# Values mixed in three reduced-precision passes, with steps of the softmax moved forward on VectorE and ScalarE

## What is computed

```python
logits = jnp.einsum('bnqhgd,bnkhd->bnhgqk', qb, kb) * (HEAD_DIM ** -0.5)
logits = jnp.where(valid, logits, -1e30)
probs = jax.nn.softmax(jnp.concatenate([logits, sink_col], axis=-1), axis=-1)[..., :-1]
out = jnp.einsum('bnhgqk,bnkhd->bnqhgd', probs.astype(v.dtype), vb)

rnn = hr * jax.nn.gelu(yr)          # hr: two gated linear recurrences, forward and backward
merged = (jax.nn.sigmoid(ga) * (attn @ w_proj_attn[i])
          + jax.nn.sigmoid(gr) * (rnn @ w_proj_rnn[i]))
```

## Time and profile before

| | us |
|---|---|
| median of three timed runs | 949.85 (949.08 to 950.12) |
| the profiled execution | 949.1 |
| its span, first to last instruction | 947.3 |
| TensorE busy | 927.0 (98%) |
| VectorE busy | 729.6 (77%) |
| ScalarE busy | 577.1 (61%) |

### The profile page before, as it was taken

The page is one execution under the profiler, slowest core; times in us unless marked ns, Lnnn a source line. Parts: engine busy times, 40 slices in busy tenths (PEclk is TensorE's granted clock), DMA queues, the critical chain, the costliest instruction groups (busy, mean ns, idle before and its releaser), DMA issues.

```text
span 947.3 us, 12574 instructions
## 1 busy us (share of the span) xinstructions
PE 927.0 (98%) x5100; PEld 800.1 (84%) x5100; DVE 729.6 (77%) x981; ACT 577.1 (61%) x730; POOL 1.4 (0%) x9
## 2 busy tenths in 40 slices
PE   5999999999999999999999999999999999999996
PEld 3898988988888888888889889888888888888885
DVE  5888898787867867767868698888878676866755
ACT  4578899764356644555345889987435564545540
POOL 0000000000000000000000000000000000000000
PEclk9999999999999999999999999999999999999998
DMA  9546444584485555566443644456656656555521
GB/s 333 153 163 200 136 156 157 185 305 164 156 266 182 199 198 178 192 203 204 160 161 119 211 159 155 134 180 197 256 179 217 226 187 205 186 180 198 201 89 45
DMA packets 118457, 174.62 MB, mean 184 GB/s; under 512 B 3968, under 2 KB 78976, under 8 KB 117888
## 3 DMA queue, kind: packets, MB, share of 16 engines
q1 hardware_dynamic: 118256, 173.79, 55.0%
q10 hardware_dynamic: 144, 0.03, 0.0%
HBM read 172.76 MB, written 1.05 MB: 183 GB/s over the span
## 4 chain that ended last, share of the span: by engine, by line
PE 88%; DVE 7%; ACT 4%; DMA 0%; issue 0%; DVEq 0%; ACTq 0%
PE ring L548 13%; PE ring L550 13%; PE ring L549 13%; PE ring L601 9%; PE ring L597 9%; PE misc L548 5%; PE misc L549 5%; PE misc L550 5%; PE ring L600 5%; PE ring L598 5%; PE misc L778 2%; DVE sb_w_lo L1253 2%; PE ring L721 1%; PE misc L837 1%; ACT sb_w_hi L933 1%; DVE sb_tmp L1485 1%
## 5 line engine op out<-in xcount | busy, mean ns | idle before, releaser
L1253 DVE TENSOR_TENSOR sb_w_lo<-sb_raw,sb_w_hi 128x2048 fp32r<-128x2048 f32 x138 | 294.8, 2148 | 65.8 <-ACT sb_w_hi L933 65.8
L933 ACT CAST sb_w_hi<-sb_raw 128x2048 fp32r<-128x2048 f32 x138 | 246.3, 1796 | 19.6 <-DMA sb_raw<-in_w_out_dram 4.3
L601 PE MATMUL ring<-sb_x_both,sb_w_hi 128*128 128x512 f32 x272 | 107.6, 396 | 0.0
L597 PE MATMUL ring<-sb_x_both,sb_w_hi 128*128 128x512 f32 x272 | 107.5, 395 | 0.0
L548 PE MATMUL ring<-sb_w_hi,sb_x_both 128*128 128x512 f32 x272 | 107.1, 394 | 0.0
L549 PE MATMUL ring<-sb_w_lo,sb_x_both 128*128 128x512 f32 x272 | 106.0, 390 | 0.0
L550 PE MATMUL ring<-sb_w_hi,sb_x_both 128*128 128x512 f32 x272 | 106.0, 390 | 0.0
L600 PE MATMUL ring<-sb_x_both,sb_w_lo 128*128 128x256 f32 x272 | 75.7, 278 | 0.0
L598 PE MATMUL ring<-sb_x_both,sb_w_lo 128*128 128x256 f32 x272 | 75.4, 277 | 0.0
L548 PE MATMUL ring<-sb_x_both,sb_w_hi 128*128 128x256 f32 x256 | 72.6, 284 | 0.0
L550 PE MATMUL ring<-sb_x_both,sb_w_lo 128*128 128x256 f32 x256 | 72.4, 283 | 0.0
(11 more groups left out here) (229 smaller groups left out, 2111.8 us busy)
## 6 DMA issues: line engine op xcount, KB each, us to landing
sb_raw<-in_w_in_dram SPq DMA_DIRECT2D x40, 1024.0 KB, 5.3
sb_raw<-in_w_up_dram SPq DMA_DIRECT2D x34, 1024.0 KB, 5.2
sb_raw<-in_w_down_dram SPq DMA_DIRECT2D x18, 1024.0 KB, 5.0
sb_raw<-in_w_proj_attn_dram SPq DMA_DIRECT2D x8, 1024.0 KB, 5.2
sb_raw<-in_w_proj_rnn_dram SPq DMA_DIRECT2D x8, 1024.0 KB, 5.1
sb_hb<-in_w_up_dram SPq DMA_DIRECT2D x8, 1024.0 KB, 5.3
sb_raw<-in_w_out_dram SPq DMA_DIRECT2D x6, 1024.0 KB, 6.2
sb_raw<-in_w_ple_gate_dram SPq DMA_DIRECT2D x6, 1024.0 KB, 5.4
```

The lines of the kernel that those rows point to most:

```text
L597: nc.tensor.matmul(bank_of(*key), hi[:, cols], x_both[:, k], start=k == 0, stop=False)
L601: last = nc.tensor.matmul(bank_of(*key), hi[:, cols], x_both[:, k + 1], start=False, stop=k + 2 == KT)
L933: nc.scalar.copy(hi_at[home][:, at], raw_at[home][:, at]).then_inc(s_hi_part, 1)
L1253: nc.vector.tensor_tensor(lo_at[home][:, 0:size], raw_at[home][:, 0:size], hi_at[home][:, 0:size].bitcast(F32), ALU.subtract).then_inc(s_s ...
```

## The change

`mix_values` uses `three` as the other products do. For that, ScalarE's copy of the turned probabilities writes fp32r (`p_hi`, in the place of `pT`), VectorE makes `p_lo` from PSUM and `p_hi` (`probs_low`, 128x1024, once a round), and once a layer ScalarE makes `v_hi` (128x512, in block ga0) and VectorE `v_lo` (`v_low`, in block ga1). The mixing waits for `probs_lo` and `v_ready` where it waited for `probs_back`. `p_lo` and `v_hi` lie in memory whose earlier content is no longer needed (parts of `qkT` and `qk`), so `probs_low` of round 0 waits for the second scores too.

Moved on VectorE: in even blocks the split of the next unit's first half goes behind `softmax_norm` and `attn_out`; in all blocks `softmax_max` goes ahead of the second split and the convolution, and `probs_low` stands behind it, also ahead of that split. Moved on ScalarE: `probs_back` goes ahead of the second split, right behind `gate_curves`; the read-out of ga1 goes ahead of `root`.

```diff
             def mix_values(l, r):
-                pe.wait_ge(s_probs_back, value("probs_back", l, r + 1))
+                pe.wait_ge(s_v_ready, value("v_ready", l, 1))
+                pe.wait_ge(s_probs_lo, value("probs_lo", l, r + 1))
                 for kb in range(TT):
-                    last = nc.tensor.matmul(misc[:, 2, :], v[:, kb, r // TT, :], pT[:, kb, :, :],
-                                            start=kb == 0, stop=kb == TT - 1)
+                    last = three(misc[:, 2, :], [x[:, kb, r // TT, :] for x in (v_hi, v_lo)],
+                                 [p_hi[:, kb, :, :], p_lo[:, kb, :, :]], kb == 0, kb == TT - 1)
...
                     gate_curves(l, i)
+                    if 3 <= i <= 6:
+                        probs_back(l, i - 3)
                     split_to(l, name, 1)
...
                     if name == "ga0":
                         qk_copies(l, [4])
-                    if 3 <= i <= 6:
-                        probs_back(l, i - 3)
+                        all_emptied(act, l, [("kv", t) for t in range(TT)])
+                        nc.scalar.copy(v_hi[:, :, :, :].rearrange("p t h d -> p (t h d)"),
+                                       v[:, :, :, :].rearrange("p t h d -> p (t h d)")).then_inc(s_v_hi, 1)
+                    if name == "ga1":
+                        unit_out(l, name)
                     if i % 2 == 1:
                         root(l, i // 2)
...
+            def probs_low(l, r):
+                dve.wait_ge(s_probs_back, value("probs_back", l, r + 1))
+                if r == 0:
+                    dve.wait_ge(s_scores, value("scores", l, TT))
+                nc.vector.tensor_tensor(p_lo[:, :, :, :].rearrange("p a g t -> p (a g t)"),
+                                        misc[:, 2:4, :].rearrange("p a n -> p (a n)"),
+                                        p_hi[:, :, :, :].rearrange("p a g t -> p (a g t)").bitcast(F32),
+                                        ALU.subtract).then_inc(s_probs_lo, 1)
...
                 for i, name in enumerate(WITH_BLOCK[1:], 1):
-                    split_to(l, name, 0)
+                    if i % 2:
+                        split_to(l, name, 0)
                     if 3 <= i <= 6:
                         softmax_norm(l, i - 3)
                     if i >= 4:
                         attn_out(l, i - 4)
+                    split_to(l, name, 0)
...
                     gate_input(l, i)
+                    if 2 <= i <= 5:
+                        softmax_max(l, i - 2)
+                    if name == "ga0":
+                        qk_lo(l, [4])
+                    if i == 3:
+                        v_low(l)
+                    if 3 <= i <= 6:
+                        probs_low(l, i - 3)
                     split_to(l, name, 1)
                     if i + 2 < 2 * RNN_BLOCKS:
                         conv(l, i + 2)
-                    if name == "ga0":
-                        qk_lo(l, [4])
-                    if 2 <= i <= 5:
-                        softmax_max(l, i - 2)
```

More of the change, by code:

```diff
@@ L238 @@
 PER = dict(
-    qk_lo_ready=5, ln_step=2 * TT * LN_STEPS, ln_norm=4 * TT, x_turned=3 * 4, x_hi=3 * 4, x_ready=3 * 4,
+    qk_lo_ready=5, probs_lo=ROUNDS, v_ready=1, v_hi=1, ln_step=2 * TT * LN_STEPS, ln_norm=4 * TT, x_turned=3 * 4, x_hi=3 * 4, x_ready=3 * 4,
     rope_step=6, qk_turned=5, qk_ready=5,
@@ L284, in hybrid_encoder @@
         lnp = sb("lnp", [P, 2, D])
-        qk = sb("qk", [P, TT, QK_HEADS, HEAD_DIM])
-        v = sb("v", [P, TT, KV_HEADS, HEAD_DIM])
-        qkT = sb("qkT", [P, QK_HEADS, SEQ], F32R)
+        qk, at = sb_at("qk", [P, TT, QK_HEADS, HEAD_DIM])
+        v_hi = again("v_hi", [P, TT, KV_HEADS, HEAD_DIM], F32R, at + 4 * KT * SEQ)
+        v, at = sb_at("v", [P, TT, KV_HEADS, HEAD_DIM])
+        v_lo = again("v_lo", [P, TT, KV_HEADS, HEAD_DIM], F32R, at)
+        qkT, at = sb_at("qkT", [P, QK_HEADS, SEQ], F32R)
+        p_lo = again("p_lo", [P, TT, GROUP, P], F32R, at)
         yg = qk[:, :, :, :].rearrange("p t h d -> p (t h d)")[:, 0:KT * SEQ].rearrange(
@@ L296, in hybrid_encoder @@
         soft = sb("soft", [P, GROUP, SEQ])
-        pT = sb("pT", [P, TT, GROUP, P])
+        pT, at = sb_at("pT", [P, TT, GROUP, P])
+        p_hi = again("p_hi", [P, TT, GROUP, P], F32R, at)
         scan_in, at = sb_at("scan_in", [P, 2, 4, SEQ])
@@ L354, in hybrid_encoder @@
         s_probs_back = sem("probs_back")
+        s_probs_lo = sem("probs_lo")
+        s_v_hi = sem("v_hi")
+        s_v_ready = sem("v_ready")
         s_mixed = sem("mixed")
@@ L1037, in probs_back @@
                 act.wait_ge(s_probs_turned, value("probs_turned", l, r + 1))
-                nc.scalar.copy(pT[:, :, :, :].rearrange("p a g t -> p (a g t)"),
+                nc.scalar.copy(p_hi[:, :, :, :].rearrange("p a g t -> p (a g t)"),
                                misc[:, 2:4, :].rearrange("p a n -> p (a n)")).then_inc(s_probs_back, 1)
@@ L1184, in _ @@
                         yr_out(l, 0, 1, ACT.Copy)
-                    elif name not in ("kv", "yr1"):
+                    elif name not in ("kv", "ga1", "yr1"):
                         unit_out(l, name)
@@ L1465, in softmax_norm, with v_low @@
                 last.then_inc(s_probs, 1)
+            def v_low(l):
+                dve.wait_ge(s_v_hi, value("v_hi", l, 1))
+                nc.vector.tensor_tensor(v_lo[:, :, :, :].rearrange("p t h d -> p (t h d)"),
+                                        v[:, :, :, :].rearrange("p t h d -> p (t h d)"),
+                                        v_hi[:, :, :, :].rearrange("p t h d -> p (t h d)").bitcast(F32),
+                                        ALU.subtract).then_inc(s_v_ready, 1)
+            def probs_low(l, r):
[6 more added lines that the diff above has]
+                                        ALU.subtract).then_inc(s_probs_lo, 1)
             def attn_out(l, r):
```

## The result

| | before | after |
|---|---|---|
| median, us | 949.07 (948.79 to 950.29, 14 runs) | 951.2 (950.61 to 953.62, 14 runs) |
| the profiled execution | 949.1 | 951.31 |
| its span | 947.3 | 949.4 |
| TensorE busy | 927.0 | 925.7 |
| VectorE busy | 729.6 | 739.2 |

The account below looks back on a forecast made before the run. TensorE, busy for 98% of the span, was taken as the bound. A layer: -1.32 (mixing) - 0.65 (ga1) + 0.35 (yr1) = -1.62; two layers -3.2, from 949.1 to 945.9 profiled, 946.6 as median; range 945.0 to 948.8.

Parts of the forecast that it names:

- The mixing: Probabilities-times-values matmuls on TensorE: a round falls from 1.71 to 1.38 us, 0.33 less, 1.32 a layer, 2.6 in the run.
- the slots: Mixing priced from the trace: six matmuls of 512 columns at 0.23 us each, 1.38 a round.
- The four-pass rule: Alternative price for the mixing: eight passes become six, 1.28 a round, 0.43 less; the sum would be 945.1.
- The wait for ga1: TensorE's gates in round 0 wait for ScalarE's ga1 read-out; the new order removes this, 0.65 us a layer.
- VectorE's prices: Added VectorE steps: `probs_low` 1.20 us once a round (1.14 and 1.36 kept as alternatives), `v_low` 0.60 once a layer.
- yr1's first half: TensorE waits 0.35 us a layer for yr1's weights, since VectorE's split moves behind the division and attention's low part.
- gr0's read-out: ScalarE in block 5: about 1.1 us later against the scores; `gates_block(6)` finds its banks at about 155.8, when wanted.
- the change doesn't do what it says: Rival: the gates' wait stays, for gr0 instead of ga1; a tenth at most, time as forecast, no chance of its own.
- The list of what would make the prediction wrong: `probs_low` far above 1.4, round 1 mixing wait over 0.5, late round 3 exponentials, or unadded waits such as `turn_probs`.

Follow-up runs that it names:

- the last run: The changed kernel with gr0's values in memory of their own and gr0 read out ahead of the root: 945.28 us, ratio 0.9962 to the kernel before.
- the first experiment: The changed kernel with the convolution, in block gr0 alone, ahead of the split of gr1's second half: 945.59 us, ratio 0.9964 to the kernel before.

## Why the prediction was wrong

**The mixing: right.** In the changed kernel the mixing of round 1 starts at 135.45 and the gates behind it at 136.81, 1.36 for a round where the slots gave 1.38.

```profile
135.45 0.39 PE L555 MATMUL misc<-sb_p_hi,sb_v_hi 128*128 128x512 f32 x1
...
136.81 0.28 PE L555 MATMUL ring<-sb_r_hi,sb_w_hi 128*128 128x256 f32 x1
```

The two kernels that differ by the passes alone lie 2.2 apart; the one with three passes has the late read-out, a quarter us a layer, so the passes are worth about 2.7, and the slots (2.6) hold. The four-pass rule of the Trainium skill ("FP8 and Floating Point Precision", section "TensorE Precision Notes") would by estimate have saved 3.4 in eight rounds, at 1.28 a round. The trace doesn't agree, with 1.36; the medians alone could not tell the two apart.

**The wait for ga1: right**, 0.65 a layer, shown by the run with the moves and the early convolution (1.3 in all), and by the list of waits. It depended on a move that the prediction hadn't connected with it: without attention's low part ahead of the split, the 0.65 comes back at `turn_probs(1)`.

**VectorE's prices: right.** In the chain `probs_low` takes 1.14 from start to start (150.02 to 151.15) for a forecast of 1.20. VectorE waits 0.93 us for the scores of round 3 where 0.9 was added up, and the hand-over is 0.20. `probs_low` of round 1 ends at 134.97 and the mixing starts at 135.45, in time by 0.34 (0.48 less 0.14 for waking) where 0.20 was forecast.

```profile
133.75 1.22 DVE L1492 TENSOR_TENSOR sb_p_lo<-misc,sb_p_hi 128x1024 fp32r<-128x1024 f32 x1
```

**yr1's first half: right in mechanism, hidden in this kernel.** In the changed kernel TensorE is 2 us late by then, so the wait can't show. It does in the last run: 0.22 for a forecast of 0.35.

**gr0's read-out: the step that failed.** The sentence that puts `gates_block(6)` at "about 155.8, just when it wants them", with "a tenth lost there", was an estimate from ScalarE's own list: split, copy, root, table, read-out. That list was nearly right: with the convolution out of the way (the first experiment) the read-out begins 6.26 behind the end of the scores (147.52 to 153.78), where it was 4.99 before (148.88 to 153.87), so 1.27 later for a forecast of 1.1. But the estimate left out what the read-out waits for on VectorE. The wait for the last convolution was in the code of the kernel before, and it never showed in the trace, since the convolution was done 0.89 ahead of the read-out (152.98 against 153.87). The prediction listed this very convolution, and what was put ahead of it, in VectorE's path to yr1: hand-over 0.20, maximum 2.30, `probs_low` 1.20, split 2.21, convolution 2.36, in all 8.27 behind the scores. With the scores' end at 147.46 in the changed kernel that is 155.73, and the read-out started at 155.75. The number was in the working and was carried to yr1 only.

On the time scale of the 155.8, where the scores end at 148.88, the convolution ends at 157.15 and the banks come free at 157.9, behind 0.61 of read-out and 0.14 for waking. Carried to the gates that is a wait of 2.1 a layer (measured 2.20) against 1.97 gained, and with it a forecast of no change, 949.1 + 2 x 0.13 = 949.4 for the profiled execution. Nothing else of weight is missing: either repair of this one wait (the convolution earlier, or gr0 in other memory) gives 945.59 and 945.63 us in the profiled executions, where 945.9 was forecast. That this comes so close is in part luck, since the quarter us that stays at the gates stands where 0.35 at yr1 was forecast.

The rival "the change doesn't do what it says" named the right place and the right wait, then dismissed it by the same incomplete sum. The list of what would make the prediction wrong looked at `turn_probs` and the exponentials, and not at the read-out.

**The clock: not priced.** Nothing in the prediction asked what an idle stretch would do to TensorE's clock. The fall adds about 1.5 us in the profiled execution, and without it the changed kernel is level with the one before (ratio 1.0007 with the stretch filled, its interval holding 1).

## What to carry to other kernels

When a step is moved on one engine, list everything that waits for its semaphore, also waits that never bind in the old trace, and above all those that guard memory laid over other memory: such a wait has no row until it costs. A finish time worked out for one reader of an engine's list must be carried to every other reader of it. An idle stretch of TensorE can cost more than its length, since the clock may fall behind it (here 1.5 us on top of 2.2), so the loss and the gain of a repair can both be larger than the wait in the list.

## What was not expected of the hardware

The granted clock fell to 0.50 for some 3.4 us behind an idle stretch of 2.0 us in layer 1 and stayed at 1.00 behind the same stretch in layer 0; at the lower level a gate matmul took a slot of 0.21 instead of 0.12, about 1.5 us in all. With 1.1 us of idle time in that place, or none, it stayed at 1.00. The run with the passes in the old order shows the same pair, 2.0 us of idle time in either layer and the fall in layer 1 alone. What sets the layers apart is open.
